# Expert outputs scattered in pair order and read back by plain loads, every second expert block turned by VectorE

## What is computed

```
scores = sigmoid(t @ router_w)                       # 640 tokens, 64 experts
_, idx = top_k(scores + router_bias, 8)
wts    = sel / sum(sel) * 2.5                        # gates of the 8 chosen
hid    = silu(t @ w_gate[e]) * (t @ w_up[e])         # 128 wide, for each chosen expert
routed = sum over the 8 of  gate * (hid @ w_down[e])
x      = x + gate2 * (routed + shared(t))            # then rmsnorm(x) * final_g
```

## Time and profile before

| | us |
|---|---|
| median of 3 runs | 1449.32 (1447.54 to 1451.58) |
| profiled execution, span | 1449.8 |
| routing, from the first logits to block 0 | about 869 to 923 |
| expert blocks 0 to 69 | 920 to 1371 |
| final sum and last norm | 1374 to 1450 |

### The profile page before, as it was taken

One profiled execution on the slowest core, in us unless ns is written; L12 is line 12 of the kernel. 1 busy time (PEld: TensorE's weight loads), 2 busy tenths in 40 slices (PEclk: granted clock), 3 DMA queues, 4 the chain that ended last, 5 costly groups with the idle time before them and its releaser, 6 DMA issues. The chain is left out here.

```text
span 1449.8 us, 21596 instructions
## 1 busy us (share of the span) xinstructions
PE 1337.0 (92%) x8160; PEld 996.5 (69%) x8160; DVE 685.5 (47%) x1254; ACT 412.0 (28%) x796; POOL 301.5 (21%) x440
## 2 busy tenths in 40 slices
PE   5999999999899998999799999999999999999664
PEld 1678666777899986555545457688888888887521
DVE  2698738202665663777576226432222222222156
ACT  3212221215556554233131025321222122212111
POOL 0200100102321311454440210211111111111173
PEclk9999999999999999999899999999999999999998
DMA  9656667121433341000120401799999999998696
GB/s 360 209 174 186 201 43 59 58 73 30 182 153 100 127 175 34 8 5 31 37 103 23 175 0 44 281 385 393 384 378 384 378 397 382 398 385 307 212 382 264
DMA packets 111005, 286.36 MB, mean 198 GB/s; under 512 B 28677, under 2 KB 46639, under 8 KB 109528
## 3 DMA queue, kind: packets, MB, share of 16 engines
q1 hardware_dynamic: 95096, 242.15, 48.6%
q0 software_dynamic: 15840, 43.28, 7.8%
HBM read 237.52 MB, written 64.56 MB: 208 GB/s over the span
## 5 line engine op out<-in xcount | busy, mean ns | idle before, releaser
L2771 PEld LDWEIGHTS PS<-arena 128*128 128x128 f32 x2240 | 258.5, 192 | 43.3 <-ACT arena L3310 26.2
L2771 PE MATMUL PS<-arena 128*128 128x128 f32 x2240 | 263.1, 276 | 5.2 <-DMA arena<-in_exp_w_down 3.9
L3098 DVE TENSOR_SCALAR arena<-PS,arena 128x1024 f32<-128x1024 f32 x70 | 89.9, 1284 | 141.6 <-PE PS L2779 141.6
L2779 PE MATMUL PS<-arena 128*128 128x512 f32 x280 | 137.8, 615 | 0.8 <-DVE arena L3091 0.8
L895 PE MATMUL PS<-arena 128*128 128x320 f32 x384 | 109.4, 438 | 1.5 <-DVE arena L1317 1.5
L3316 ACT ACTIVATE arena<-PS 128x128 f32<-128x128 f32 x70 | 19.4, 277 | 312.7 <-issue 176.7
L900 PE MATMUL PS<-arena 128*128 128x320 f32 x384 | 107.3, 432 | 0.0
L3091 DVE TENSOR_TENSOR arena<-arena,PS 128x128 f32<-128x128 f32 x70 | 20.1, 288 | 182.8 <-ACT arena L3316 93.4
L895 PEld LDWEIGHTS PS<-arena 128*128 128x128 f32 x384 | 73.0, 192 | 33.3 <-issue 2.9
L900 PEld LDWEIGHTS PS<-arena 128*128 128x128 f32 x384 | 73.0, 190 | 30.4
L3403 POOL DMA_INDIRECT arena<-h_rows,arena x70 | 72.1, 1030 | 58.4 <-POOL arena L3400 57.6
(11 more groups left out here) (478 smaller groups left out, 2078.0 us busy)
## 6 DMA issues: line engine op xcount, KB each, us to landing
arena<-in_exp_w_gate SPq DMA_DIRECT2D x70, 512.0 KB
arena<-in_exp_w_up SPq DMA_DIRECT2D x70, 512.0 KB
arena<-in_exp_w_down SPq DMA_DIRECT2D x70, 512.0 KB
y_rows<-arena SPq DMA_DIRECT2D x70, 512.0 KB
arena<-in_w_in SPq DMA_DIRECT2D x16, 1024.0 KB, 6.2
arena<-in_w_mod SPq DMA_DIRECT2D x32, 512.0 KB, 3.7
y_rows<-cst SPq DMA_DIRECT2D x2, 5632.0 KB, 18.5
y_rows<-cst SPq DMA_DIRECT2D x2, 5120.0 KB, 18.0
```

Of the source, the lines that this page charges most:

```text
L2771: mm = pe.matmul(PS[:, bank, 0:P], w[:, k, :], xT[j % 2][:, k, :], start=k == 0, stop=k == KT - 1)
L2779: mm = pe.matmul(PS[:, 4 + 2 * (j % 2) + half, :], hid[j % 2], ed[j][:, 512 * half:512 * half + 512], start=True, stop=True)
L3098: dve.tensor_scalar(yb[j].rearrange("p (h n) -> p h n", h=2), PS[:, 4 + 2 * (j % 2):6 + 2 * (j % 2), :], gate_col[j % 2], None, ALU.mult). ...
```

## The change

It does the following:
- **Rows.** The table holds the number of the pair (8 x token + choice, `pair_less`) instead of the token; `token_row` is its eighth, rounded, and `pair_row` the number itself. The multiplication of `at_block` moves from ACT to POOL.
- **Scatter.** The result of a block is evicted by ACT without its gate (`take_y`, Copy) and stored by POOL with an indirect DMA to row `pair_row` of `y_rows`, only for filled slots. `y_rows` is now in the order of pairs, 5120 rows.
- **Final sum.** SP reads result rows back with plain loads, one of 128 rows (a row of 4 KB each 32 KB) for each t and k. The gates come in here: `gates_of` collects them on DVE in the loop (blocks 5 to 9), ACT makes scaled identities for PE (`weigh_out`) and takes choice 0, DVE adds choices 1 to 3 with scalar_tensor_tensor.
- **Quarter rows.** For every second block (j odd) POOL gathers four times 128 quarter rows of 1 KB, so that a 32x32-block transpose on DVE (`turn_x`) gives `xT`. PE transposes only even blocks. The list of quarter rows needs four more PE matmuls (`spread_ident`, `slots`) behind the shared expert's.
- **Order.** Blocks 0 to 65 are unrolled; blocks 66 to 69 run in the loop (`LEAST` 3). PE's order in a block is gate/up b, transposes b+1, down b-1. `gact` has two buffers, gate and up share a bank.
- The gates' columns of `h2_rows` and the constant fill of `y_rows` are gone.

The diff, cut to its core:

```diff
-                    q = slice((COLS - NE) * (i - 1) // (PAIRS1 - 1), (COLS - NE) * i // (PAIRS1 - 1))
-                    sp.dma_start(y_spill[:, q], spread(at["strict"][:, 0:D], 1, q.stop - q.start)).then_inc(tail_out, 16)
...
-        LEAST = 2
+        LEAST = 3
+        FIXED = NE + 2
+        FULL = NE // U
...
+        VECTOR = tuple(j % 2 == 1 for j in range(U))
...
-                with sp.Fori(1, NE // U) as i:
-                    for j in range(U):
-                        sp.wait_ge(e_ps, U * i + (j + 1 - U))
-                        load_block(U * i + j, j)
-                        store_block(U * i + (j - U), j)
+                for b in range(U, NE):
+                    sp.wait_ge(e_ps, b - U + 1)
+                    load_block(b, b % U)
...
+                for b in range(NE, FIXED):
+                    spill_load(b - NE, b % U, b - U + 1)
                 with sp.Fori(1, groups) as i:
                     for j in range(2):
                         spill_load(2 * i + j, j, 2 * i + (NE - 1 + j))
-                        store_block(2 * i + (NE - 2 + j), j)
...
+                for n in range(PAIRS):
+                    t, k = n // TOPK, CHOICES[n % TOPK]
+                    if n >= GB:
...
+                    sp.dma_start(back[n % GB], y_pairs[:, t, k]).then_inc(g_in[n % GB], 16)
...
+                pe.wait_ge(m_slots, 2)
+                for g in range(4):
+                    mm = pe.matmul(PS[:, 7, COLS * g:COLS * g + COLS], spread_ident[g].rearrange("p a s -> p (a s)"), slots, start=True, stop=True)
+                mm.then_inc(m_rows, 1)
...
+                for b in range(FIXED):
+                    gate_up(b % U, b // U + 1, by_vector(b), by_tensor(b))
+                    if b + 1 < FIXED and by_vector(b + 1) is None:
+                        transpose_x(b + 1, (b + 1) % U, fetched(b + 1))
+                    if b:
+                        down(b - 1, (b - 1) % U, b <= 2)
...
+                dve_order.done(dve.tensor_scalar(halved, PS[:, 6, 0:COLS], TOPK * TOK - (TOPK - 1) / 2, 1.0 / TOPK, ALU.add, ALU.mult))
+                dve_order.done(dve.tensor_scalar(halved, halved, MAGIC, None, ALU.add))
+                dve.tensor_scalar(token_row, halved, -MAGIC, None, ALU.add).then_inc(m_tok, 1)
...
+                def turn_x(b):
+
+                    j = b % U
+                    dve.wait_ge(e_x[j], fetched(b))
+                    if b >= 2:
+                        dve.wait_ge(e_gu, b - 1)
+                    dve.transpose(xT[j % 2].rearrange("p k (g s) -> p g k s", s=32),
+                                  xg[j].rearrange("p g (i k) -> p g k i", i=32)).then_inc(e_turn, 1)
...
+                for b in range(FIXED):
+                    hidden(b, b % U, b < 2)
+                    if b + 2 < FIXED and by_vector(b + 2) is not None:
+                        turn_x(b + 2)
+                    if b < NT:
+                        own(b)
+                    elif b < 2 * NT:
+                        gates_of(b - NT)
...
+                for b in range(FIXED):
+                    silu(b, b % U, b < 2)
+                    if b + 1 < FIXED and by_tensor(b + 1) is not None:
+                        copy_xT((b + 1) % U, by_tensor(b + 1))
+                    if b:
+                        take_y(b - 1, (b - 1) % U, 16 * ((b - 1) // U) if b > U else None)
...
+                for t in range(NT):
+                    pool.wait_ge(m_beq, t + 1)
+                    pool.tensor_tensor(at_block[t % 2], at_block[t % 2], spread(pair_less[:, t * TOPK:(t + 1) * TOPK], 2, COLS),
+                                       ALU.mult).then_inc(m_bl, 1)
...
+                    for g in range(4):
+                        pool.indirect_dma_start(xg[j][:, g, :], None, T["h2_rows"], bass.IndirectOffsetOnAxis(rows[:, g:g + 1], 0),
+                                                bounds_check=4 * TOK - 1, oob_is_err=False).then_inc(e_x[j], 16)
...
+                    pool.indirect_dma_start(T["y_rows"], bass.IndirectOffsetOnAxis(rows, 0), yb[j], None,
+                                            bounds_check=TOPK * TOK - 1, oob_is_err=False).then_inc(e_out[j], 16)
...
+                LAG = 5
+                for b in range(FIXED):
+                    fetch(b)
+                    if b >= LAG:
+                        store(b - LAG)
```

More of the change, by code:

```diff
@@ L3149, in _ @@
                 for t in range(NT):
-                    first, second = choice(t, 0), choice(t, 1)
-                    dve.tensor_tensor(acc[:, t, :], first, second, ALU.add).then_inc(g_dve, 2)
-                    if t > 0:
-                        last_mean(t - 1)
-                    for k in range(2, 4):
-                        third = choice(t, k)
-                        dve.wait_ge(g_dve, 4 * t + k)
-                        dve.tensor_tensor(acc[:, t, :], acc[:, t, :], third, ALU.add).then_inc(g_dve, 1)
+                    for k in range(1, 4):
+                        row = choice(t, k)
+                        if k == 1:
+                            dve.wait_ge(g_first, t + 1)
+                        else:
+                            dve.wait_ge(g_dve, 3 * t + k - 1)
+                        dve.scalar_tensor_tensor(out=acc[:, t, :], in0=row, scalar=gate_of[:, t, k:k + 1], in1=acc[:, t, :],
+                                                 op0=ALU.mult, op1=ALU.add).then_inc(g_dve, 1)
+                        if k == 1 and t > 0:
+                            last_mean(t - 1)
                     if t > 0:
@@ new lines, in spill @@
+                def spill(i, before, free):
+                    copy_xT(0, 2 * i + SPILL_T)
+                    take_y(2 * i + (NE - 1), before, free)
+                    silu(2 * i + NE, 0)
+                    copy_xT(1, 2 * i + (SPILL_T + 1))
+                    take_y(2 * i + NE, 0, 16 * i + 16 * FULL)
+                    silu(2 * i + (NE + 1), 1)
+                groups = group_count(act)
+                with act.Fori(1, groups) as i:
+                    spill(i, 1, 16 * i + 16 * (FULL - 1))
@@ new lines, in _, with weigh_out, first_choice @@
+                take_y(2 * groups + (NE - 1), 1, 16 * groups + 16 * (FULL - 1))
+                def weigh_out(t):
+                    for k in range(4, TOPK):
+                        i = act.activation(weigh[4 * t + k - 4], ident, ACT.Copy, scale=gate_of[:, t, k:k + 1])
+                    i.then_inc(g_diag, 1)
+                def first_choice(t):
+                    n = TOPK * t
+                    act.wait_ge(g_in[n % GB], 16 * (n // GB + 1))
+                    act.wait_ge(f_own, NT)
+                    act.activation(acc[:, t, :], back[n % GB], ACT.Copy, scale=gate_of[:, t, 0:1]).then_inc(g_first, 1)
@@ new lines, in store, with fetch_spill @@
+                def store(b):
+                    if b == 0:
+                        pool.wait_ge(m_tok, 2)
+                    pool.wait_ge(e_y, b + 1)
+                    scatter(b % U, pair_row[:, b:b + 1])
+                LAG = 5
[3 more added lines that the diff above has]
+                        store(b - LAG)
+                def fetch_spill(i, j, free, transposed):
+                    block, copied = 2 * i + (NE + j), 2 * i + (j - 1)
+                    pool.compute_val(block)
+                    pool.compute_val(copied)
+                    pool.wait_ge(free, transposed)
+                    pool.tensor_copy(token_col[j], token_row[:, bass.ds(block, 1)]).then_inc(x_col, 1)
+                    pool.wait_ge(h2_out, 16 * NT)
+                    pool.wait_ge(x_col, copied)
+                    gather_rows(j, token_col[j])
@@ new lines, in _ @@
+                groups = group_count(pool)
+                for j in range(2):
+                    store(FIXED - LAG + j)
+                    if VECTOR[j]:
+                        fetch_spill(1, j, e_turn, by_vector(NE + j))
+                    else:
+                        fetch_spill(1, j, e_tr, by_tensor(NE + j))
+                for b in range(FIXED - LAG + 2, FIXED):
+                    store(b)
+                with pool.Fori(2, groups) as i:
+                    for j in range(2):
+                        fetch_spill(i, j, e_tr, 2 * i + (SPILL_T - 2 + j))
+                        store_spill(i - 1, j)
@@ L3437 @@
+                for j in range(2):
+                    store_spill(groups - 1, j)
 _IN = ['x_prompt', 'x_sample', 'c', 'state_gdn', 'state_hgrn', 'state_mlstm_c', 'state_mlstm_n',
```

315 lines of the change are left out of this document (154 added, 161 removed).

## The result

The changed kernel takes 1474.5 us (median of 4 runs, 1473.5 to 1479.9) against 1448.4 us of the kernel before in the same session (1446.7 to 1451.6): a ratio of 1.018, 95% interval 1.016 to 1.020. It is 26 us slower, where the prediction had 27 us faster. Its profiled execution spans 1471.7 us (before: 1449.8).

A forecast was written before the change was run, and what follows sets the result against it. It took TensorE and DMA both as limits of the expert loop; loop -28.7, start +5.9, section +3.3, handover +0.5, final sum -8 gave -27.0 us, from 1449.3 to 1422 us, range 1406 to 1440.

The forecast's parts named there:

- loop, DMA side: Expert-block loop: even block 5.71 us, odd 5.96, mean 5.83 of DMA; 5.85 taken, -28.7 us over 63 blocks.
- PE side: Expert-block loop: odd blocks lose their PE transposes, 0.87 us each, so TensorE needs 5.80 us a block.
- Rival C: Loop: 1 KB packets cost 110 ns, not 57, so DMA stays the bound at the old pace; 1451 us, chance 0.07.
- D: Loop: 1 KB packets cost more than 113 ns; at 125 ns +37 us, 1459 us; chance 0.06.
- B: Loop: VectorE's turn locks out GpSimd, whose issue becomes the bound; 6.05 us a block, +12.6, 1435 us; chance 0.14.
- E: Loop: the turn on VectorE takes over 5.6 us; at 6 us +45 us, 1467 us; chance 0.04.
- The loads on SP ... nothing waited there: Loop: SP's loads lose the store behind which the next load waited; claimed nothing waited there, no cost.
- Start: Start of the expert stage: table product on GpSimd and late quarter list; gate/up(0) +4.5, block 1 +6, term +5.9 us.
- Section of blocks 66 to 69: Blocks with weights by table: load of 66 waits for the later down(64); +3.3 us, bounds -2 to +5.
- Final sum: End of kernel: plain loads of result rows replace gathers, 54 us instead of 62.2; -8 us, bounds -2 to -11.
- Handover: After the last blocks: eviction on ScalarE 1.0 instead of 1.28 us, scatter issue 1.0 us more; +0.5 us.
- Fill: Constant fill of y rows removed: it runs under the scans and holds nobody; 0.

The follow-up runs named there:

- even_store: Changed kernel with the first 66 blocks stored whole by plain transfers instead of scattered (final sum reads wrong rows): 1450.4 us.
- early loads: Changed kernel, gate and up weights loaded after gate/up of b-4, down weights after down of b-4: 1462.7 us; with slots spread too: 1433.3 us.
- pe_first: Changed kernel with slots spread and early loads, plus blocks 1 and 3 gathered by whole rows and turned by TensorE: 1410.6 us.
- all_blocks_pe: Changed kernel with every block gathered as whole rows and transposed by PE, no quarter rows or VectorE turn: 1483.3 us.
- order_all: Changed kernel with indirect stores writing all 128 slots of a block side by side (final sum reads wrong rows): 1470.9 us.
- order_filled: Changed kernel with indirect stores writing only filled slots, to row 128 b + slot (final sum over wrong rows): 1475.0 us.

## Why the prediction was wrong, point by point

**The step that failed: loop, DMA side.** It said (384 + 72 + 72) x 173 / 16 = 5.71 us. The packets were counted rightly, the division by 16 was wrong. It holds where every engine gets its sixteenth, as with the kernel before's whole-block stores; the change took 56 store packets a block off, nearly all of them from engines that were not the bound. The engines of the low slots kept 24 + 8 + 8 = 40, 6.2 us at 155 ns, and even_store, which has just these, ran at 6.19. The other 0.43 us came with the scatter onto the same engines; I had put nothing for it beyond its packets, and why it costs that is open. Spreading the slots gives 5.863 with early loads, against my 5.85, and 5.735 in pe_first, against my PE side of 5.80. So the two prices I compared came within 2% for a kernel whose rows are spread, the DMA side with some luck: its odd block had 288 x 57 ns for quarter rows that the records show as 72 x 159. The loop holds 48 of the 53 us between forecast and result; spreading gives back 37 (63 x 0.59), early loads with it 11 (63 x 0.17), of which some 7 are the hole at block 51. The hint was in the trace of before: gathers that took as long for 46 rows as for 98. The Trainium skill states the rule, and I had not weighed it.

**Rival C and D** had the right place, DMA, and the wrong reason. The quarter rows are no short packets: in the records those of four neighbouring partitions in one gather stand as one of 4096 B at 159 ns, and only where a neighbouring slot is empty are there pieces (1036 B 47 ns, 2056 B 85 ns, 3076 B 122 ns). The four gathers of block 1, with 54 filled slots, left 52 of 4096 B, four of 2056 B and 72 of 16 B. all_blocks_pe without them is slower. **B** fell: GpSimd was busy 21.24 of 40 us and waited 168.1 us for evictions; and the lock that it feared did not show, for during the turn from 931.1 to 933.1 us GpSimd issued gathers at 931.6 and 932.9 in 1.0 us each, as ever. **E** fell: 2.02 us a turn, inside my 1.3 to 2.5, PE waited for a turn once, in block 1.

**"The loads on SP ... nothing waited there".** Wrong in one part: TensorE's new order puts down(b-1) behind gate/up(b), so a load starts up to a block later. I saw this for the section of blocks 66 to 69 and not for the loop. Early loads, together with down weights that gate/up needn't wait for, were worth 0.11 us a block with the slots low, 7 us, and 0.06 to 0.17 with them spread.

**Start.** gate/up(0) was right (+5.0, forecast +4.5), and its mechanism in the main: the tables wait for GpSimd. But I had the delay grow over five rounds, and it comes with the first two: counted from the logits, the second table starts 36.5 instead of 31.0 us after them (+5.5), the last 47.9 instead of 42.6 (+5.3). Block 1 was mis-sized, +12.0 at gate/up(2) against +5.9:

```profile
931.09 2.01 DVE L3136 STREAM_TRANSPOSE arena<-arena 128x1024 f32<-128x1024 f32 x1 [10.70 <-DMA arena<-h_rows,arena]
```
```profile
933.24 6.41 PE L2807 MATMUL PS<-arena 128*128 128x128 f32 x32 [6.88 <-DVE arena L3136]
```

Counted from the logits, the first quarter gather was issued after 57.5 us (921.2), as forecast (926, 57 after the logits of the kernel before). The turn came after 67.4 us (931.1), where I had 65 (934): from first issue to turn it was 9.9 us and not 8. With that gate/up(1) started 9.4 us later than before, against my +6. And then, after 6.88 us of idleness, it took 6.41 instead of the 3.73 us that it took before, 2.7 more. The table by stretches, 920 to 940 us, before and after:

```profile
920.00:940.00 20.00, 18.26 (x137) 16.20 (x138) 10.40 (x15) 3.90 (x6) 6.45 (x9) 1.00 1.01 389
```
```profile
920.00:940.00 20.00, 11.70 (x77) 11.41 (x78) 4.93 (x6) 1.58 (x3) 14.03 (x14) 0.74 0.88 323
```

The granted clock falls to 0.74 in the mean; behind that pause, from 933.24 to 936.5 us, it is 0.50, 1.2 instead of 2.4 GHz. I had the wait a little short, and not what the wait does to TensorE. all_blocks_pe (71.5 us to gate/up(2)) and pe_first (70.5), which don't wait for a turn there, show the size of both together: 7 to 8 us.

**Section of blocks 66 to 69**: +5.6 against +3.3, mechanism right. The load of 66 goes out at 1364.70, after down(64), and gate/up(66) starts at 1371.55, 12.5 us after gate/up(65) (I had 12.6); it takes 5.46 instead of 3.73 us after its own wait:

```profile
1371.55 5.46 PE L2807 MATMUL PS<-arena 128*128 128x128 f32 x32 [4.41 <-DMA arena<-in_exp_w_down]
```

**Final sum**: -9.1 against -8, right in size and cause. From the first load's issue to the last data in use it takes 54.2 us (1405.46 to 1459.61; forecast 54), at 410 GB/s, near the best of the earlier trace rows:

```profile
1426.00:1436.00 10.00, 7.89 (x16) 2.71 (x16) 8.68 (x9) 3.64 (x5) 0.00 (x0) 1.00 1.03 410
```

**Handover**: -1.0 against +0.5. **Fill** and **unrolling**, both 0: no run tested them alone.

**The ranges.** The bound I gave the loop, 5.80 to 5.95, came from two prices of the same kind. A bound on how evenly the work is shared was missing, and C and D, which would have covered a loop of 6.3 to 6.4, had 0.13 together.

## What to carry to other kernels

- A DMA share is a mean over engines. Before a transfer of part of the rows replaces a whole one, count the packets of the fullest engine. A share that falls while matmuls wait for transfers was, here, the sign that one group of engines was the bound.
- Where slots fill from the low end, lay slot k out so that consecutive slots fall on different engines: one table, 0.59 us of 6.62 a block here, and with early loads and TensorE taking the first blocks it turns +1.8% into -2.7% (1410.6 us).
- Before a difference between two traces is put down to an edit, compare it with the spread of the runs: the loops of order_all and order_filled differ by 11 us, their medians by 4.
- Look at every wait that hangs on an order that changed, the loads' too, and let the first rounds, where nothing is fetched ahead, keep the short path.

## What the runs showed of the hardware

- A gather with skipped rows takes the time of its fullest engine: 2.9 us for 46 rows of 4.3 KB in low slots, 1.2 us for the same rows spread; in low slots 1.3 us for 32 rows and 2.3 for 37.
- With uneven slots, an indirect store of all 128 rows of a block costs more than a plain one (1470.9 against 1450.4 us); with the slots spread, the scatter costs no more than plain stores (1438.9 against 1438.4). Skipping the empty slots saved nothing with uneven slots (1475.0 us), though it moves fewer bytes.
- In an indirect gather of 1 KB rows, those of four neighbouring partitions leave one packet of 4096 B, 159 ns, which is what one row of 4 KB takes.
- A turn of 128x1024 fp32 in 32x32 blocks is 2.02 us on VectorE, against 1.28 us of a plain pass.
- GpSimd's product of 848 elements is 2.52 us alone, and 4.93 us for two beside VectorE's comparisons; the comparisons took 2.37 and 2.62 us beside it instead of 1.04 and 1.22.
